# Input turned and split without its norm in both layers of a two-layer attention trunk: the root applied when products are copied out

## What is computed

```python
def rms_norm(x, g):
    xf = x.astype(jnp.float32)
    y = xf * lax.rsqrt(jnp.mean(xf * xf, axis=-1, keepdims=True) + EPS) * g.astype(jnp.float32)

def stick_breaking_layer(x, norm_g, w_in, w_out):
    h = rms_norm(x, norm_g)
    q, k, v, gate = jnp.split(h @ w_in, 4, axis=-1)
    ...
    return (jax.nn.silu(gate) * o) @ w_out

def shared_kv(x, kv_norm_g, w_kv, k_norm_g, cos, sin):
    h = rms_norm(x, kv_norm_g)
    k, v = jnp.split(h @ w_kv, 2, axis=-1)
    ...
def diff_layer(x, k, v, norm_g, w_in, ...):
    h = rms_norm(x, norm_g)
    q, gate = jnp.split(h @ w_in, 2, axis=-1)
    ...
```

## Time and profile before

| | |
|---|---|
| median of 3 runs | 653.1 us |
| profiled execution | 652.19 us |
| its span, first to last instruction | 650.9 us |
| PE busy | 624.5 us, 3,324 products |
| DVE, ACT, POOL busy | 448.4, 334.5, 350.8 us |
| chain that ended last | PE 71%, DVE 18%, ACT 5%, issue 4% |
| bytes read from HBM | 44.5 MB, 72 GB/s over the span |

### The profile page before, as it was taken

The page is one execution under the profiler, slowest core; times in us unless marked ns, Lnnn a source line. Parts: engine busy times, 40 slices in busy tenths (PEclk is TensorE's granted clock), DMA queues, the critical chain, the costliest instruction groups (busy, mean ns, idle before and its releaser), DMA issues.

```text
span 650.9 us, 9998 instructions
## 1 busy us (share of the span) xinstructions
PE 624.5 (96%) x3324; PEld 527.8 (81%) x3324; DVE 448.4 (69%) x701; ACT 334.5 (51%) x728; POOL 350.8 (54%) x339
## 2 busy tenths in 40 slices
PE   5899999999999999999999999999899999998998
PEld 4788778888888888888877888788688888886876
DVE  3486177979788797883236398515779999998531
ACT  5352184675747667484326535323466754665320
POOL 4556396546565465643442454448655577554251
PEclk9999999999999999999999999999899999999999
DMA  7433122112121121211110222232321221131141
GB/s 255 106 103 98 49 83 81 49 48 64 47 81 48 48 64 34 84 45 65 65 65 33 98 97 90 88 98 54 101 74 49 81 81 27 54 98 49 32 162 64
DMA packets 61773, 49.08 MB, mean 75 GB/s; under 512 B 7728, under 2 KB 48816, under 8 KB 61744
## 3 DMA queue, kind: packets, MB, share of 16 engines
q1 hardware_dynamic: 58064, 48.25, 24.0%
q10 hardware_dynamic: 3680, 0.46, 0.5%
HBM read 44.50 MB, written 2.10 MB: 72 GB/s over the span
## 4 chain that ended last, share of the span: by engine, by line
PE 71%; DVE 18%; ACT 5%; issue 4%; DMA 1%; DVEq 0%; POOL 0%; SPq 0%; ACTq 0%
PE bank L586 19%; PE bank L588 18%; PE bank L587 18%; PE bank L700 6%; PE bank L714 3%; PE bank L685 2%; DVE hi L1468 2%; ACT pr L1301 2%; DVE small L1665 1%; DVE pr L1686 1%; DVE h_hi L1431 1%; DVE v L1383 1%; DMA xs<-in_x 1%; DVE lo L1473 1%; ACT v L986 1%
## 5 line engine op out<-in xcount | busy, mean ns | idle before, releaser
L477 POOL TENSOR_TENSOR w_lo<-w_raw,w_hi 128x512 fp32r<-128x512 f32 x100 | 143.5, 1435 | 8.0
L465 POOL TENSOR_TENSOR w_lo<-w_raw,w_hi 128x512 fp32r<-128x512 f32 x60 | 81.8, 1370 | 121.4 <-ACT w_hi L1001 121.3
L475 POOL CAST w_hi<-w_raw 128x512 fp32r<-128x512 f32 x100 | 74.8, 748 | 130.4 <-DVE pr L1686 37.6
L586 PE MATMUL bank<-w_hi,h_hi 128*128 128x512 f32 x320 | 128.6, 402 | 5.8 <-DVE h_lo L1389 2.8
L586 PE MATMUL bank<-h_hi,w_hi 128*128 128x512 f32 x320 | 129.7, 405 | 2.7 <-ACT q L1213 1.5
L588 PE MATMUL bank<-w_hi,h_lo 128*128 128x512 f32 x320 | 125.9, 394 | 0.0
L588 PE MATMUL bank<-h_hi,w_lo 128*128 128x512 f32 x320 | 125.8, 393 | 0.0
L587 PE MATMUL bank<-w_lo,h_hi 128*128 128x512 f32 x320 | 125.8, 393 | 0.0
L587 PE MATMUL bank<-h_lo,w_hi 128*128 128x512 f32 x320 | 125.6, 393 | 0.0
L586 PEld LDWEIGHTS bank<-w_hi,h_hi 128*128 128x128 f32 x320 | 60.7, 190 | 19.3 <-DVE h_lo L1389 3.5
L586 PEld LDWEIGHTS bank<-h_hi,w_hi 128*128 128x128 f32 x320 | 60.5, 189 | 17.0 <-ACT q L1213 1.4
(11 more groups left out here) (174 smaller groups left out, 1197.3 us busy)
## 6 DMA issues: line engine op xcount, KB each, us to landing
w_raw<-in_a_w_in SPq DMA_DIRECT2D x64, 256.0 KB, 2.8
w_raw<-in_w_kv SPq DMA_DIRECT2D x32, 256.0 KB, 3.0
w_raw<-in_b_w_in SPq DMA_DIRECT2D x32, 256.0 KB, 2.8
w_raw<-in_a_w_out SPq DMA_DIRECT2D x16, 256.0 KB, 2.7
w_raw<-in_b_w_out SPq DMA_DIRECT2D x16, 256.0 KB, 2.9
xs<-in_x SPq DMA_DIRECT2D x4, 512.0 KB, 5.2
qrot<-qs SPq DMA_DIRECT2D x32, 64.0 KB, 2.0
out_x<-xs SPq DMA_DIRECT2D x8, 256.0 KB, 2.6
```

The costliest lines, as they stand in the source:

```text
L465: nc.gpsimd.tensor_tensor(w_lo[s][:, :], w_raw[s][:, :], w_hi[s][:, :].bitcast(F32), ALU.subtract).then_inc(s_w, 1)
L475: nc.gpsimd.tensor_copy(w_hi[s][:, :], w_raw[s][:, :]).then_inc(s_whi, 1)
L477: nc.gpsimd.tensor_tensor(w_lo[s][:, :], w_raw[s][:, :], w_hi[s][:, :].bitcast(F32), ALU.subtract).then_inc(s_w, 1)
L586: pe.matmul(o, ahi, bhi, start=start, stop=False, skip_group_check=True)
```

## The change

1. Layer A: PE turns the raw rows `xs` directly, each row tile when it has landed, with 4 or 8 small products behind each (`BUSY_A`). ACT and DVE split what is turned, times the gain, into `h2_hi`/`h2_lo`. No rows are normed.
2. Keys, values and layer A's values are products of that unnormed input, and take the row's root as the scale of the activation (or the DVE operation) that copies them out.
3. q, k and gate of layer A, and q and gate of layer B, need a normed input in `h1_hi`/`h1_lo`. ACT keeps a float32 copy of each turned tile (`input_raw`, `sum_raw`). PE turns the roots, spread over 128 columns (`turn_roots`), and ACT copies them to `og`. DVE multiplies copy by roots (`query_scale`), ACT rounds (`query_hi`), DVE subtracts (`query_lo`), over two buffers `g32` and `ge`.
4. Layer B: the sum is turned inside the output projection (`turn_sum(0)` after step 1 of its second half) and after step 1 of the first key/value group (`turn_sum(1)`), in banks by `TURN_BANK` and `KV_BANK`. The 14 unread products are gone.
5. The gain's load moves from SP to ACT's queue, ahead of everything; `load_params` moves from behind input tile 3 to behind tile 7.

The diff, cut to what is spoken of below:

```diff
-BUSY_A, BUSY_B = 30, 14
+BUSY_A = [4, 8, 4, 8]
+TURN_BANK = [7, 6, 1, 2, 3, 4, 5, 0]
+KV_BANK = [1, 2, 6, 7, 0, 3, 4, 5, 1, 2, 0, 3, 4, 5, 1, 2]
...
+        def turn_roots(n, o):
+            pe.wait_ge(s_rx, n + 1)
             for t in range(TT):
+                tr = pe.transpose(o[:, cols(t * P, P)], rx[:, t:t + 1].to_broadcast([P, P]), ident[:, :])
+            tr.then_inc(s_rt, 1)
...
-        keep_busy(neg_one[:, :], BUSY_A)
-        turn_input(0, 4, 0, 0)
+        for t in range(TT):
+            pe.wait_ge(s_x[t], 16)
+            for k in range(4):
+                turn_input(k, t)
+            keep_busy(neg_one[:, :], BUSY_A[t])
...
-        pe.wait_ge(s_x2, TT)
-        keep_busy(h2_hi[:, 0, :], BUSY_B)
-        turn_input(0, 4, 1, 0)
+            if k == 1:
+                turn_sum(0)
...
+        def input_raw(k):
+            act.wait_ge(s_h, k + 1)
+            A(raw_input(0, k), bank[4 + k % 4][:, :], ACT.Copy, scale=gain[:, 0, k:k + 1]).then_inc(s_raw, 1)
+        def query_hi(n, k):
+            act.wait_ge(s_f, n * KT + k + 1)
+            A(h1_hi[:, k, :], (g32, ge)[k % 2][:, :], ACT.Copy).then_inc(s_hh, 1)
...
+        for k in range(4):
+            input_hi(k)
+        for k in range(4):
+            input_raw(k)
+        squares(0, TT - 1, 0)
+        squares(0, TT - 1, 1)
+        root(tiny[:, 0:4], tiny[:, 4:8], R_A)
+        for k in range(4, KT):
+            input_hi(k)
+            if k == 6:
+                roots_copy(0, bank[7])
+            input_raw(k)
+            slab_hi(v_slab(RING_A + k - 4))
+        load_params()
         for k in range(KT):
+            query_hi(0, k)
+            if k in (1, 3, 5):
+                slab_hi(v_slab(10 + k // 2))
...
+        def query_scale(n, k):
+            dve.wait_ge(s_raw, n * KT + k + 1)
+            dve.wait_ge(s_rc, n + 1)
+            if k >= 2:
+                dve.wait_ge(s_h, (2 * n + 1) * KT + k - 1)
+            TTN((g32, ge)[k % 2][:, :], raw_input(n, k), og[:, :], ALU.mult).then_inc(s_f, 1)
+        def query_lo(n, k):
+            dve.wait_ge(s_hh, (2 * n + 1) * KT + k + 1)
+            TTN(h1_lo[:, k, :], (g32, ge)[k % 2][:, :], h1_hi[:, k, :].bitcast(F32), ALU.subtract).then_inc(s_h, 1)
```

More of the change, by code:

```diff
@@ L1008, in root, with input_hi, roots_copy @@
             A(dst, dst, ACT.Exp, scale=-0.5).then_inc(s_ry, 1)
[L1010 to L1016, removed]
+        def input_hi(k):
+            act.wait_ge(s_tp, k + 1)
+            A(h2_hi[:, k, :], bank[4 + k % 4][:, :], ACT.Copy, scale=gain[:, 0, k:k + 1]).then_inc(s_hh, 1)
+        def input_raw(k):
+            act.wait_ge(s_h, k + 1)
+            A(raw_input(0, k), bank[4 + k % 4][:, :], ACT.Copy, scale=gain[:, 0, k:k + 1]).then_inc(s_raw, 1)
+        def roots_copy(n, src):
+            act.wait_ge(s_rt, n + 1)
+            A(og[:, :], src[:, :], ACT.Copy).then_inc(s_rc, 1)
+        def query_hi(n, k):
+            act.wait_ge(s_f, n * KT + k + 1)
+            A(h1_hi[:, k, :], (g32, ge)[k % 2][:, :], ACT.Copy).then_inc(s_hh, 1)
+        with nc.allow_non_contiguous_dma(reason="one column per feature tile"):
+            nc.scalar.dma_start(gain[:, 0, :], a_norm_g.rearrange("o (k p) -> p (o k)", p=P)).then_inc(s_gain, 16)
         nc.scalar.preload_act_table_set("natural_log_exp_and_others")
-        for t in range(TT):
+        for t in range(TT - 1):
             squares(0, t, 0)
             squares(0, t, 1)
-        root(tiny[:, 0:4], tiny[:, 4:8], R_A)
-        norm_last_rows(0)
         def load_params():
@@ L1060, in values_a @@
             bulk_tile(act, v_slab((n // TT + 1) * KT - 1) + 1, n)
-            A(v32[:, n % TT, cols(n // TT * HALF, HALF)], bank[n % 6][:, :], ACT.Copy).then_inc(s_vk, 1)
-        for n in (10, 11, 12):
-            slab_hi(v_slab(n))
+            A(v32[:, n % TT, cols(n // TT * HALF, HALF)], bank[n % 6][:, :], ACT.Copy,
+              scale=rx[:, n % TT:n % TT + 1]).then_inc(s_vk, 1)
         for n in range(TT):
@@ L1183, in _, with sum_hi, sum_raw @@
         slab_hi(G_OUT + 15)
[L1184 to L1187, removed]
+        def sum_hi(k):
+            act.wait_ge(s_tp, KT + k + 1)
+            act.wait_ge(s_wu, G_OUT + KT + k + 1)
+            A(h2_hi[:, k, :], bank[TURN_BANK[k]][:, :], ACT.Copy, scale=gain[:, 1, k:k + 1]).then_inc(s_hh, 1)
+        def sum_raw(k):
+            act.wait_ge(s_h, 2 * KT + k + 1)
+            A(raw_input(1, k), bank[TURN_BANK[k]][:, :], ACT.Copy, scale=gain[:, 2, k:k + 1]).then_inc(s_raw, 1)
         def bulk_copy(n):
@@ L1228, in kv_hi @@
                 slab_hi(kv_slab(n))
[L1231 to L1235, removed]
+        for k in range(TT):
+            sum_hi(k)
+        for k in range(TT):
+            sum_raw(k)
+        for t in range(TT):
+            squares(1, t, 1)
+        kv_hi(4)
+        root(tiny[:, 0:4], tiny[:, 4:8], R_B)
+        kv_hi(5)
+        for k in range(TT, KT):
+            sum_hi(k)
+        kv_hi(6)
+        for k in range(TT, KT):
+            sum_raw(k)
+        kv_hi(7)
+        roots_copy(1, bank[3])
+        kv_hi(8)
+        query_hi(1, 0)
+        query_hi(1, 1)
+        kv_hi(9)
+        query_hi(1, 2)
+        query_hi(1, 3)
+        kv_hi(10)
+        query_hi(1, 4)
+        query_hi(1, 5)
+        act.wait_ge(s_f, KT + TT)
         for n in range(4):
@@ L1378, in norm_rows, with input_lo, query_input @@
             newton(tiny[:, 0:4], tiny[:, 4:8], tiny[:, 8:12], rx, R_A + n).then_inc(s_rx, 1)
[L1379 to L1394, removed]
+        def input_lo(k):
+            dve.wait_ge(s_hh, k + 1)
+            STT(out=h2_lo[:, k, :], in0=bank[4 + k % 4][:, :], scalar=gain[:, 0, k:k + 1], op0=ALU.mult,
+                in1=h2_hi[:, k, :].bitcast(F32), op1=ALU.subtract).then_inc(s_h, 1)
+        def query_scale(n, k):
[7 more added lines that the diff above has]
+            TTN(h1_lo[:, k, :], (g32, ge)[k % 2][:, :], h1_hi[:, k, :].bitcast(F32), ALU.subtract).then_inc(s_h, 1)
+        def query_input(n):
+            query_scale(n, 0)
+            for k in range(KT):
+                if k + 1 < KT:
+                    query_scale(n, k + 1)
+                query_lo(n, k)
+        for k in range(4):
+            input_lo(k)
+        row_roots(0)
+        for k in range(4, KT):
+            input_lo(k)
+        query_input(0)
         def q_lo_a(n):
```

113 lines of the change are left out of this document (68 added, 45 removed).

## The result

| | before | with the change |
|---|---|---|
| median, runs beside each other | 653.39 us (651.19 to 653.76, 4 runs) | 662.79 us (661.52 to 663.37, 4 runs) |
| profiled execution, its span | 652.19, 650.9 us | 663.37, 662.1 us |
| ratio of after to before, 95% interval | | 1.0153, 1.0133 to 1.0173 |

The account below looks back on a forecast made before the run. It took TensorE, busy 96% of the span, to bound the kernel. Slab 8's stand 2.4, clock 1.9 and between the layers 1.3 made 5.6 on the profiled 652.2: 657.8 us, range 642 to 662 (forecast's own 654 to 662).

Parts of the forecast that it names:

- The first rotated keys came 10.1 us after it: Layer 2's keys: from DVE's first reduction at about 371.0, 10.1 us as before, to first rotated keys at 381.0.
- First product: Start of layer 1: PE's first real product at 13.0, ends 12.5 and 13.5, 7.4 us before 20.40.
- Issue of the parameters: ACT in layer 1: issuing 14 parameter DMAs takes 8.4 us, from 29.7 to 38.1, ahead of the query highs.
- rival (b): Slab 8, layer 1: the value copy is in time and the kernel faster, 643.1 or 639.9 us; chance 0.24.
- (c): Start of layer 1: no earlier start, as the gain's load shares DMA engines with the rows; no separate chance given.
- 9.9: Layer 1, DVE and ACT taking turns over two buffers: 9.9 us with two highs and one value copy, to 48.0.
- 1.0 for two of them: Layer 1: two of three w_lo slow DVE's query work by 1.0 each; slab 8's product starts at 50.0, +2.4.
- Clock after the stand: Layer 1 behind PE's stand of 9.4 us: the lowered clock costs +1.9 us, ends 0 and 3.0.
- Between the layers: From output projection to layer 2's second keys: 5.3 us won by step 12, then late keys leave +1.3; ends -2.1, +3.2.
- The clock after the 5 us stand: Layer 2, behind PE's wait for first keys: no clock loss in the sum; a lowered clock only in the +3.2 end.
- 4.7 us after the first: Layer 2: second keys come 4.7 us after the first, as before, so PE waits 1.6 us again.
- Rival (a): Both layers: gains and new waits cancel, DVE and POOL hardly meet, the clock holds; 650.5 us, chance 0.28.

## Why the prediction was right, and where it was off

The sign, both places and the kinds of cause came as forecast. The size did not: +11.2 us on the profile for +5.6, and the median 0.8 us over the top of the range. The step that failed most lies at the keys of layer 2: "The first rotated keys came 10.1 us after it" (it took 12.0), together with the clock behind PE's stand there, which I had put at nothing in the sum (it cost 2.3). In layer 1 two terms were mis-sized.

1. *First product* 13.23 for 13.0, right. Step 0 at full clock was only an end of the range; it was the case, so PE stood from 39.3 and not 40.6. This alone moves no time, as all waits at slab 8 anyway.
2. *Issue of the parameters* 29.41 to 37.79 for 29.7 to 38.1. The length, 8.4, was right, and rival (b), the copy in time, is refuted, as is (c). The start was luck. I let PE set it, with its last turns done at 28.1. They were done at 27.2 (26.53 and 0.63), and what set the start was ACT and DVE: high, low, raw copy and slab high of one tile came 2.6 us behind those of the one before (the lows at 23.33, 25.93 and 28.54).
3. *"9.9" and "1.0 for two of them":* two mis-sized terms. From the first high to the product without meetings is 10.6 (37.89 to 48.51), 0.7 of hops between the engines more than I added; and all three meetings count, 1.06 each: 3.2, not 2.0. I had argued the third "mostly past the last scaling"; its slab high stands before the last two query highs, and DVE's low at 47.73 met it. With the issue over 0.3 sooner, +2.4 became +4.0.
4. *Clock after the stand* 2.5 for 1.9. At the start eight intervals were of 0.43; here eleven were. The dummies show that the stand did it. Layer 1: +6.5 for +4.3, and 6.8 at DVE's first additions to the stream; where the last 0.3 came from stays open.
5. *Between the layers:* projection, first group, turned roots and key squares (376.43, which less 6.8 is 369.6, for 369.8) came to within 0.2 us, and the first reduction (377.95 less 6.8 is 371.2) as well, for 371.0. Then the failed step. The interval of 10.1 was one of before, with two meetings of DVE and POOL in it (374.69 and 377.06). At its new place it held four, since the slabs had been used and their highs came in a row. With the highs spread out one was left, and it took 8.9.
6. *The clock after the 5 us stand* was an end of my range and should have been in its middle: I had written that a stand of 9 us costs clock, and took 0 for one of 5. It cost 2.3, as the 22 dummies show.
7. *The second keys "4.7 us after the first":* they came 2.7 after them (391.99 and 0.69), with no w_lo beside them, so the wait of 1.6 would not have come at full clock either: with the dummies the second turn ran 3.27 behind the first, without a wait. So keys 2.2 later, clock 2.3, second turn 1.4 sooner behind the first: +1.3 became +4.3 (0.1 of it is the old time, 384.52, which I had taken 0.1 too early).

The sum is 4.0 + 2.5 + 0.3 + 4.3 = 11.1 at the second turn, and 11.2 at the end. My upper end, "652.2 + 7 + 3", was not added up either: the ends that I gave for the terms (2.4 + 3.0 and 3.2) make 8.6. The gains of the change were real, 8.3 us up to slab 8 and 5.7 between the layers; both were spent in a stand at the next thing that ACT and DVE owed, now queued behind the new query work. Rival (a) had the clock hold and the meetings rare; neither was so. One wait was not forecast at all, the 1.76 us for slab 12; it cost nothing, as PE only stood less for the keys.

By the rule of the Trainium skill cited above (page "SBUF — State Buffer", section "Who interferes with whom"), the operation that starts later waits for the whole of the other. The trace agrees: the low of 43.81 ended at 45.56, 0.54 after POOL's operation that had started 0.08 before it (43.73 to 45.02), and alone such a low takes 0.69. By my 1.29 for each of three meetings the sum would be 3.9, against 3.2 measured.

## What to carry to other kernels

When an early gain sends an engine ahead, follow it to the next buffer it needs and list everything that now stands in front of the instruction that frees it, DMA issues included; the gain is worth what that queue leaves. Give each stand of the matrix engine its price in clock as well, not as an end of the range. And an interval measured before holds only where its neighbours are the same: count anew which of POOL's operations fall beside DVE's. An order in the program that did not change can still run differently, when what it waited for is now there.

## What I had not expected

**The last part does not take the same time twice.** From layer 2's first rotated query to the last additions, all these kernels run the same code. Yet this stretch, from DVE's first product of the rotation (0.61 before the times given for that query above) to the start of the last additions, took from 212.6 to 216.0 us in 13 profiles (before 213.4, after 213.5). The clock fell some 30 to 40 us into it in ten of them and some 155 to 170 us into it in three, two of which are among the ten; two profiles, with 212.6 and 212.7, had no fall. Stretches at the same distances from that query (from:to, us, PE busy, granted clock, DMA share, GB/s), first of the kernel with the slab highs behind the copies, then of the one with 50 dummies:

```profile
469.80:474.80 5.00, 3.71 (x22) 1.00 0.25 73
474.80:479.80 5.00, 4.29 (x35) 1.00 0.08 18
599.80:604.80 5.00, 4.22 (x21) 1.00 0.00 1
```

```profile
471.60:476.60 5.00, 1.94 (x9) 0.77 0.11 34
476.60:481.60 5.00, 5.00 (x29) 0.89 0.13 31
601.60:606.60 5.00, 3.65 (x11) 0.74 0.16 56
```

The second was 2.2 us ahead of the changed kernel at its first rotated query (442.20 for 444.37) and took 2.5 longer from there, 216.0 for 213.5. The clock is not all of it: both orders of layer 1 mended took 215.0 with one fall and 1.4 us more idle time of PE than the changed kernel (3.08 for 1.72) between 50 and 150 us into it, and with layer 2 mended as well it was 212.6, also with one. What decides whether a given gap lowers the clock stays open; filling those late gaps was not tried. For a gain of 2 us the time at a milestone behind the edit says more than the total.
